# Down-projection weights of three mixtures read in runs of four rows per partition, and the experts' activations turned by VectorE

## The reference, cut to what matters

```python
for e in range(N_EXPERTS):                       # first block: 32 experts, w_gate[e] is 1024x512
    h = jax.nn.silu(t @ w_gate[e]) * (t @ w_up[e])
    y = y + combine[:, e:e + 1] * (h @ w_down[e])          # w_down[e] is 512x1024
...
# second block, in both layers: 16 experts, w_gate[e] is 1024x1024, 32 tokens chosen for each
a = jax.nn.silu(jnp.einsum('becd,edf->becf', xs, w_gate)) * jnp.einsum('becd,edf->becf', xs, w_up)
y = jnp.einsum('becf,efd->becd', a, w_down) * g[..., None]
```

## Time and profile before

| | |
|---|---|
| median of 3 runs | 1899.59 us (1899.16 to 1899.98) |
| span of the profiled execution | 1899.5 us |
| TensorE matmuls busy | 1436.6 us (76%) |
| VectorE busy | 473.1 us (25%) |
| ScalarE busy | 245.5 us (13%) |
| read from HBM | 714.6 MB, 377 GB/s over the span |
| 2 MB loads of expert weights from SP: M1 | 96 |
| the same, M2[0] and M2[1] together | 192 |

### The profile page before, as it was taken

How to read it: one execution, slowest core, us unless ns; L and a number is a source line. 1 busy time by engine, 2 the same in 40 slices (tenths; PEclk the granted TensorE clock), 3 DMA queues, 4 the chain that set the end, 5 groups by cost and what they waited for, 6 DMA issues and landing times.

```text
span 1899.5 us, 30837 instructions
## 1 busy us (share of the span) xinstructions
PE 1436.6 (76%) x13698; PEld 813.9 (43%) x13698; DVE 473.1 (25%) x938; ACT 245.5 (13%) x616; POOL 83.0 (4%) x92
## 2 busy tenths in 40 slices
PE   9899996677687889999666556667999756566565
PEld 5455542333243354666333223225866423323322
DVE  4764421111112048942000000003553100000001
ACT  2233220111211112321000000001001000000000
POOL 2210000000000023200000000000000000000000
PEclk9999998989899999999877888878999988878978
DMA  9445999999999988489999999999997999999997
GB/s 363 174 178 207 364 400 423 420 421 419 419 417 415 416 331 321 174 361 386 422 422 418 424 419 422 420 420 397 363 395 312 418 420 422 419 424 420 421 421 303
DMA packets 123098, 717.72 MB, mean 378 GB/s; under 512 B 5968, under 2 KB 10832, under 8 KB 98384
## 3 DMA queue, kind: packets, MB, share of 16 engines
q1 hardware_dynamic: 121536, 713.11, 92.4%
q10 hardware_dynamic: 1424, 2.56, 0.4%
HBM read 714.60 MB, written 1.05 MB: 377 GB/s over the span
## 4 chain that ended last, share of the span: by engine, by line
DMA 55%; PE 34%; DVE 5%; issue 2%; POOL 2%; ACT 1%; SPq 0%; DVEq 0%; ACTq 0%; POOLq 0%
DMA ring<-in_moe_w_up 36%; DMA ring<-in_w_down 14%; PE bank L1653 6%; PE bank L506 5%; PE bank L2554 4%; PE bank L1703 3%; DMA ring<-in_moe_w_down 3%; PE bank L1644 2%; PE bank L340 2%; PE bank L970 1%; PE bank L1001 1%; PE bank L650 1%; DMA ring<-in_w_gate 1%; PE bank L2314 1%; PE bank L1731 1%
## 5 line engine op out<-in xcount | busy, mean ns | idle before, releaser
L1653 PE MATMUL bank<-ring,arena 128*32 128x256 f32 x3840 | 288.1, 454 | 173.4 <-DMA ring<-in_moe_w_up 103.0
L1703 PE MATMUL bank<-ring,arena 128*32 128x256 f32 x2976 | 231.0, 463 | 169.9 <-DMA ring<-in_moe_w_down 127.0
L1653 PEld LDWEIGHTS bank<-ring,arena 128*32 128x32 f32 x3840 | 141.5, 126 | 299.2 <-issue 113.8
L1703 PEld LDWEIGHTS bank<-ring,arena 128*32 128x32 f32 x2976 | 114.3, 129 | 277.9 <-issue 165.9
L1644 PE MATMUL bank<-ring,arena 128*32 128x512 f32 x976 | 131.7, 661 | 59.7 <-DMA ring<-in_w_up 33.6
L506 PE MATMUL bank<-ring,low 128*128 128x512 f32 (+1 forms) x352 | 156.7, 597 | 2.5 <-DMA ring<-in_w_in 2.5
L1777 DVE TENSOR_TENSOR arena<-arena,bank 128x128 f32<-128x128 f32 (+1 forms) x64 | 22.7, 355 | 519.0 <-PE bank L1653 515.3
L1731 PE MATMUL bank<-arena 32*128 32x256 f32 x1024 | 92.5, 431 | 15.0 <-PE bank L1731 10.6
L506 PEld LDWEIGHTS bank<-ring,low 128*128 128x128 f32 x352 | 67.8, 199 | 72.8 <-issue 71.5
L1783 ACT ACTIVATE arena<-bank 128x256 f32<-128x256 f32 x64 | 24.6, 385 | 548.9 <-PE bank L1717 548.9
L1792 DVE TENSOR_TENSOR arena<-bank,gate_strips 128x256 f32<-128x256 f32 x32 | 13.6, 425 | 283.9 <-PE bank L1703 283.9
(11 more groups left out here) (319 smaller groups left out, 1392.9 us busy)
## 6 DMA issues: line engine op xcount, KB each, us to landing
ring<-in_moe_w_up SPq DMA_DIRECT2D x62, 2048.0 KB, 26.5
ring<-in_moe_w_down SPq DMA_DIRECT2D x62, 2048.0 KB, 27.2
ring<-in_moe_w_gate SPq DMA_DIRECT2D x58, 2048.0 KB, 25.5
ring<-in_w_up SPq DMA_DIRECT2D x31, 2048.0 KB, 26.0
ring<-in_w_down SPq DMA_DIRECT2D x31, 2048.0 KB, 26.2
ring<-in_w_gate SPq DMA_DIRECT2D x30, 2048.0 KB, 26.6
ring<-in_ada_w SPq DMA_DIRECT2D x24, 2048.0 KB, 13.3
ring<-in_attn_w_in SPq DMA_DIRECT2D x8, 2048.0 KB, 21.1
```

Of the source, the lines that this page charges most:

```text
L1653: last = nc.tensor.matmul(GU[up][32 * j:32 * j + 32, 0:QW], xgT[:, x + kk, a:a + C], w[:, kq, j * QW:(j + 1) * QW], start=(kk == 0), stop= ...
L1703: last = nc.tensor.matmul(z_bank(M)[32 * j:32 * j + 32, 0:QW], act_s[:, b, q * C:(q + 1) * C], w[:, kq, j * QW:(j + 1) * QW], start=(kk == ...
```

## The change

The down weights are laid out like the gate and up weights: partition p gets four whole rows that follow each other (in M1 rows 4p to 4p+3; in M2 rows 8p to 8p+7, in two loads of four). The activations must then lie on the partitions in the same order. ScalarE's silu writes `silu_s` with its columns reordered (column 4m+k goes to 32k+m in M1, 8m+k in M2), and the multiply reads the up part in that order. Then VectorE transposes each block of 32x32 of `silu_s` straight into `act_s` (`turn_act_dve`). The transposes on TensorE, the PSUM half they used and ScalarE's copy are gone. Waits that went over the removed copy now go over the new turn, or over what used to be implied: `sums_pe` waits for the multiply of the expert before, `w_turn_pe` for ScalarE's copy of the combine weights.

```diff
@@ -1300,7 +1300,7 @@
         xgT = carve(2 * KD, GE * C)
         wsel = carve(2 * T, GE * C)
         silu_s = carve(2 * P)
-        act_s = carve(2, P)
+        act_s = carve(KD, C)
         z_s = carve(QW)
         scaled = carve(T, GE * C)
         wselT = carve(2, S)
...
@@ -1657,6 +1657,8 @@
         def sums_pe(M, k, e, up, r):
 
             pe = nc.tensor
+            if e:
+                pe.wait_ge(M.act, nth(M, e, 1, r, k))
             if up:
                 pe.wait_ge(M.u_dve, nth(M, e + 1, 1, r, k))
             elif M is M1 and so_far(CTX_TURN, e):
...
@@ -1672,22 +1674,13 @@
             if up:
                 last.then_inc(M.turned, 1)
 
-        def act_turn_pe(M, k, e, r):
-
-            pe = nc.tensor
-            pe.wait_ge(M.act, nth(M, e + 1, 1, r, k))
-            pe.wait_ge(M.wT, nth(M, e + 1, 1, r, k))
-            for b in range(M.nf):
-                last = nc.tensor.transpose(WT[:, S + b * P:S + (b + 1) * P], silu_s[:, b * P:(b + 1) * P], ident)
-            last.then_inc(M.a_turned, 1)
-
         def z_bank(M):
             return bank[2] if M.nf == 2 else bank[0]
 
         def down_pe(M, k, e, r):
 
             pe = nc.tensor
-            pe.wait_ge(M.a_copied, nth(M, e + 1, 1, r, k))
+            pe.wait_ge(M.a_turned, nth(M, e + 1, 1, r, k))
             if e < M.ne - 1 and M.nf == 1:
                 pe.wait_ge(M.g_act, nth(M, e + 2, 1, r, k))
             nk = 4 * M.nf
...
@@ -1711,7 +1703,7 @@
             if e % GE == 0:
                 pe.wait_ge(M.wsel, nth_group(M, 2 * (g + 1), 2, r, k))
             if e:
-                pe.wait_ge(M.a_copied, nth(M, e, 1, r, k))
+                pe.wait_ge(M.wT, nth(M, e, 1, r, k))
             for t in range(T):
                 for j in range(4):
                     last = nc.tensor.matmul(WT[32 * j:32 * j + 32, t * P:(t + 1) * P], wsel[:, (g % 2) * T + t, a:a + C], ident,
...
@@ -1698,9 +1691,8 @@
                 w = wait_moe_item(pe, M, i, r, k).rearrange("p (k n) -> p k n", n=D)
                 for kq in range(4):
                     kk = 4 * part + kq
-                    q, b = divmod(kk, M.nf)
                     for j in range(4):
-                        last = nc.tensor.matmul(z_bank(M)[32 * j:32 * j + 32, 0:QW], act_s[:, b, q * C:(q + 1) * C],
+                        last = nc.tensor.matmul(z_bank(M)[32 * j:32 * j + 32, 0:QW], act_s[:, kk, :],
                                                 w[:, kq, j * QW:(j + 1) * QW], start=(kk == 0), stop=(kk == nk - 1))
                 last.then_inc(M.done, 1)
 
...
@@ -1751,15 +1743,12 @@
                 v.wait_ge(M.turned, nth(M, e, 1, r, k))
             v.tensor_copy(up_s, GU[1][:, :]).then_inc(M.u_dve, 1)
 
-        def copy_act_act(M, k, e, r):
-
-            nc.scalar.wait_ge(M.a_turned, nth(M, e + 1, 1, r, k))
-            if e:
-                nc.scalar.wait_ge(M.z, nth(M, e, 1, r, k))
-            nc.scalar.activation(act_s[:, 0:M.nf, :], WT[:, S:S + M.nf * P].rearrange("p (b c) -> p b c", c=P), ACT.Copy).then_inc(M.a_copied, 1)
-
         def gate_up(M):
             return (SUMS[:, 0:P], SUMS[:, P:2 * P]) if M.nf == 1 else (GU[0][:, 0:QW], GU[1][:, 0:QW])
+
+        def by_rows(M, a, pattern):
+
+            return a.rearrange(pattern, m=C, k=M.w // C)
 
         def silu_act(M, k, e, r):
             if M.nf == 1:
...
@@ -1768,13 +1757,20 @@
                 nc.scalar.wait_ge(M.done, nth(M, M.done0 + place_up(M, e, 0, 1) + 1, M.per, r, k - M.k0))
             if e:
                 nc.scalar.wait_ge(M.a_turned, nth(M, e, 1, r, k))
-            nc.scalar.activation(silu_s[:, 0:M.w], gate_up(M)[0], ACT.Silu).then_inc(M.silu, 1)
+            nc.scalar.activation(by_rows(M, silu_s[:, 0:M.w], "p (k m) -> p m k"), by_rows(M, gate_up(M)[0], "p (m k) -> p m k"),
+                                 ACT.Silu).then_inc(M.silu, 1)
 
         def mul_dve(M, k, e, r):
             nc.vector.wait_ge(M.silu, nth(M, e + 1, 1, r, k))
             if M.nf == 2:
                 nc.vector.wait_ge(M.done, nth(M, M.done0 + place_up(M, e, 1, 1) + 1, M.per, r, k - M.k0))
-            nc.vector.tensor_tensor(silu_s[:, 0:M.w], silu_s[:, 0:M.w], gate_up(M)[1], ALU.mult).then_inc(M.act, 1)
+            prod = by_rows(M, silu_s[:, 0:M.w], "p (k m) -> p k m")
+            nc.vector.tensor_tensor(prod, prod, by_rows(M, gate_up(M)[1], "p (m k) -> p k m"), ALU.mult).then_inc(M.act, 1)
+
+        def turn_act_dve(M, k, e, r):
+
+            nc.vector.wait_ge(M.act, nth(M, e + 1, 1, r, k))
+            nc.vector.transpose(act_s[:, 0:M.w // C, :].rearrange("p k c -> p (k c)"), silu_s[:, 0:M.w]).then_inc(M.a_turned, 1)
 
         def copy_wT_act(M, k, e, r):
             nc.scalar.wait_ge(M.w_turned, nth(M, e + 1, 1, r, k))
...
@@ -1860,6 +1852,7 @@
             mul_dve(M, k, e, r)
             if e and M.nf == 2:
                 copy_z_dve(M, k, e - 1, r)
+            turn_act_dve(M, k, e, r)
             if e % GE == 1 and e < M.ne - GE:
                 select_dve(M, k, e // GE + 1, r, looped)
             if e % GE == 2 and e < M.ne - GE:
...
@@ -1986,13 +1977,13 @@
 
         def src1(what, x, n):
             if what == 2:
-                return w_down[0, x].rearrange("(k p) n -> p k n", p=P)
+                return w_down[0, x].rearrange("(p k) n -> p k n", p=P)
             return (w_up if what else w_gate)[0, x].rearrange("(p k) n -> p k n", p=P)
 
         def src2(l):
             def src(what, x, n):
                 w = (moe_w_gate, moe_w_up, moe_w_down)[what][l, x]
-                return w.rearrange("(k p) n -> p k n" if what == 2 else "(p k) n -> p k n", p=P)[:, 4 * n:4 * n + 4, :]
+                return w.rearrange("(p k) n -> p k n", p=P)[:, 4 * n:4 * n + 4, :]
             return src
 
         main = (arrived, item_done)
```

More of the change, by code:

```diff
@@ L53, in __init__ @@
         (self.sel, self.wsel, self.staged, self.gathered, self.xg_act, self.xg_dve, self.g_act, self.u_dve,
-         self.turned, self.silu, self.act, self.a_turned, self.a_copied, self.z, self.w_turned, self.wT, self.y, self.y_added) = steps
+         self.turned, self.silu, self.act, self.a_turned, self.z, self.w_turned, self.wT, self.y, self.y_added) = steps
 def rope_tables(ang, half):
@@ L1496, in transformer_blocks @@
         STEPS = ("sel", "wsel", "staged", "gathered", "xg_act", "xg_dve", "g_act", "u_dve", "turned", "silu", "act",
-                 "a_turned", "a_copied", "z", "w_turned", "wT", "y", "y_added")
+                 "a_turned", "z", "w_turned", "wT", "y", "y_added")
         kind1, kind2 = ([sem(f"{kind}_{n}") for n in STEPS] for kind in ("m1", "m2"))
```

6 lines of the change are left out of this document (removed).

## The result

The changed kernel takes 1874.67 us (median of 4 runs, 1873.87 to 1879.4) against 1899.56 before (4 runs, 1899.16 to 1899.98): a ratio of 0.9875, with 95% between 0.9861 and 0.9889. The two profiled executions differ by 26.9 us (spans of 1899.5 and 1872.6).

A forecast was written before the change was run, and what follows sets the result against it. Only the DMA engines were taken to set the pace in the mixtures. 87 down loads at 0.21 us, less 0.2, gave 18.1 us, all other terms 0: 1899.5 - 18.1 = 1881.4, predicted 1881.5 us; range 1877 to 1888.

The forecast's parts named there:

- A down load costs 0.21 us more; 87 of them, 18.1 us.: In the mixtures' unbroken loading, 87 down loads each lose 0.21 us against gate and up loads; 18.1 us in sum.
- The nine early loads: Nine down loads before unbroken loading begins, covered by TensorE's own work and the routing; no gain counted.
- Transposes, copy, reordered columns, new waits: 0.: In the mixtures, removed TensorE transposes and ScalarE copies, reordered access and new waits hide behind waits for loads; 0 us.
- The turn, estimate 0.45 us (0.29 to 1.34), cost 0.: VectorE's transpose in the mixtures, taken as 0.45 us, fits in 2.3 us of room at M1's last expert; cost 0.
- the sum itself: Whole kernel: profiled execution 1899.5 less 18.1 gives 1881.4 us.
- the span stand 0.1 us from its own time: Whole kernel: the profiled execution's span was taken to lie 0.1 us from the median, making 1881.4 into 1881.5 us.
- A: Rival, down loads: only half of the 0.21 us comes from run length; 9.1 us gained, 1890.4 us; chance 0.06.
- B: Rival, mixtures: rare steps of 1.6 us come from short packets and go; 13.2 us more, 1868.3 us; chance 0.05.
- C: Rival, down loads: runs still cut to 4 KB, or another limit near 410 GB/s; time stays 1899.5 us; chance 0.03.
- D: Rival, convolution behind a mixture: TensorE's clock rises later, up to 42 us longer, 1923 us; chance 0.03.
- The range's low end, 1877: Whole kernel: 1899.5 less 19.1 (0.22 us per load) less 3.2 (steps of 1.6 us twice less) gives 1877 us.

The follow-up runs named there:

- turn_only: The changed kernel with the down weights read in the old order, 4 KB runs; 1895.02 us, ratio 0.9981 to the kernel before.
- before_front24: The kernel before with 24 instructions more (waits already met) at the start of VectorE's program; 1895.6 us, ratio 0.9979 to the kernel before.
- the second measurement: The changed kernel, unchanged, measured once more against the kernel before, at 1899.18 us there; 1876.32 us, ratio 0.988.

## Why the prediction was wrong, step by step

- *A down load costs 0.21 us more; 87 of them, 18.1 us.* Right. The mixtures gave 18.0 us between the two profiles and 18.4 with the loads alone. M2[0] gave 6.5 to 7.5 and M2[1] 6.2 to 6.5 (6.3 forecast for each, 30 x 0.21), M1 4.3 to 5.4 (5.7 forecast, 27 x 0.21). That the sum agrees to 0.1 us is in part luck, since M1 alone spreads by 3 us from profile to profile. The nine early loads gave nothing that can be told from the clock's chance.
- *Transposes, copy, reordered columns, new waits: 0.* Right in the mixtures: 1332.45 us with the turn and 1332.37 without.
- *The turn, estimate 0.45 us (0.29 to 1.34), cost 0.* Right. It takes 311 ns in M1 and 435 ns in M2; silu with reordered columns takes 392 and 604 ns instead of 278 and 378, and the multiply stays at 288 and 421. The groups by line and shape, after:

```profile
L1760 ACT ACTIVATE arena<-bank 128x256 f32<-128x256 f32 x32 | 19.3, 604 | 222.8 <-PE bank L1653 222.8
L1773 DVE STREAM_TRANSPOSE arena<-arena 128x256 f32<-128x256 f32 x32 | 13.9, 435 | 0.1
...
L1760 ACT ACTIVATE arena<-bank 128x128 f32<-128x128 f32 x32 | 12.6, 392 | 214.8 <-PE bank L1672 214.8
L1773 DVE STREAM_TRANSPOSE arena<-arena 128x128 f32<-128x128 f32 x32 | 10.0, 311 | 1.1
```

- *The step that failed is the sum itself*, 1899.5 - 18.1. It has a term for each instruction that the change adds or removes, and none for where the others then stand. Outside the mixtures it takes 0. There the changed program stops VectorE's stall at the jump behind M1. That is worth 5.2 us (3.3 of VectorE's waiting, 1.7 of TensorE's clock behind it, 0.2 open); `turn_only` and `before_front24` show 4.3 of it, since TensorE's clock dips in both ahead of the next gather. The row with 5.33 us of "issue" was in the trace of before, ahead of the chain of norms that block 2 starts with. I read the chain and the waits only inside the mixtures.
- *The rest of the 26.9 us:* 3.8 us before the first gather, a matter of the clock in one execution. Nor did the span stand 0.1 us from its own time, as I took it: in every run here with both numbers the time is 1.8 to 2.0 us above the span (1874.42 against 1872.6). So the profiled execution of before was about 1.8 us slower than the median, and the medians differ by 24.9 us, in the second measurement by 22.9. Loads and jump make 22.3 to 23.6. Even the second measurement, 1876.32 us, lies below the range.
- *Rivals.* A (half of 0.21): no, the mixtures gave twice its 9.1 us. B (the late steps of 1.6 us go with the short packets): no. From the second down product of M2[0] to its last, 80 loads now take 396.22 us against 80 x 4.90 = 392.0, 4.2 us of steps where 4.4 were. C: no. D: no, between M2[0] and M2[1] every kernel takes 148.2 to 148.5 us; behind M1 the clock did change, but for the better, as the stall went. The range's low end, 1877, came from loads and steps alone, and so missed 1874.67.

## What to carry to other kernels

Where the DMA engines set the pace, count packets: a 2 MB load in 4 KB runs costs 4% more than one in 16 KB runs, and a trace of the kernel before already shows it load by load. Before costing an edit at nothing outside its stage, look at every jump and loop behind it for idle time marked "issue": an edit that adds or removes instructions shifts the code, and can start or stop such a stall of 4 to 5 us, as 24 idle instructions did here. To tell the parts of a change from chance, profile both kernels twice and compare stretch by stretch.

## What the runs showed of the hardware beyond that

VectorE's stall hangs on the place of a jump: seven of nine tried places have it, two neighbours (24 and 40 instructions later) don't, though the code gives a hint to fetch 23 instructions ahead of the jump. Moving the target by 48 or by 80 places changed nothing. The stall ends 1.67 to 1.74 us after an 8 KB packet of code has landed, in ten profiles of ten. Behind the stall TensorE's wait cost more than itself: behind 3.27 us of waiting 16 matmuls took 5.38 us, behind 0.69 us they took 3.69. TensorE's clock in the first 35 us is not the kernel's own: the same program was granted 1.00 in one execution and 0.50 in another between 15 and 17.5 us, and with a second such dip reached its first gather 3.4 us later. ScalarE pays for writing reordered columns (392 ns against 278), VectorE doesn't for reading them (288 and 288).
